# Merge-gate weights of a split-precision decoder block: the low half of every second weight tile by an accumulating DMA

## What is computed

```python
h = rmsnorm(x, g_norm)
z = einsum('bsd,dn->bsn', h, w_in)          # 16 heads' q/k/v/gate, forget logits, two merge gates
qa, ka, va, ga, qb, kb, vb, gb, fl, ma, mb = split(z)
...                                         # differential and forgetting attention, gated by SiLU
ya = einsum('bsw,wd->bsd', oa, w_proj_a)
yb = einsum('bsw,wd->bsd', ob, w_proj_b)
m = sigmoid(ma) * ya + sigmoid(mb) * yb
x = x + einsum('bsd,de->bse', m, w_out)
return rmsnorm(x, g_final)
```

## Time and profile before

| | |
|---|---|
| median of 3 runs | 762.3 us (762.3 to 762.76) |
| the profiled execution, its own time | 762.72 us |
| its span, first to last instruction | 760.9 us |
| PE busy | 751.2 us, 99% of the span |
| DVE busy | 422.1 us, 55% |
| ACT busy | 365.8 us, 48% |
| POOL busy | 76.3 us, 10% |
| bytes moved | 143.80 MB, 189 GB/s over the span |
| mean granted TensorE clock | 0.998 of full speed |

### The profile page before, as it was taken

How to read it: one execution, slowest core, us unless ns; L and a number is a source line. 1 busy time by engine, 2 the same in 40 slices (tenths; PEclk the granted TensorE clock), 3 DMA queues, 4 the chain that set the end, 5 groups by cost and what they waited for, 6 DMA issues and landing times.

```text
span 760.9 us, 9586 instructions
## 1 busy us (share of the span) xinstructions
PE 751.2 (99%) x3632; PEld 628.7 (83%) x3632; DVE 422.1 (55%) x616; ACT 365.8 (48%) x556; POOL 76.3 (10%) x153
## 2 busy tenths in 40 slices
PE   8999999999999999999999999999999999999996
PEld 6898888888888888888888888888888888888886
DVE  6754555555555566566665564444445666565552
ACT  6563554445544555445545554443444443444541
POOL 0001111101121221122202000000000000001110
PEclk9999999999999999999999999999999999999999
DMA  8747554554555545554545555555555555855642
GB/s 315 267 159 257 175 185 165 169 191 166 182 174 171 177 166 171 179 178 164 184 166 167 178 173 183 189 192 194 194 194 193 192 180 193 347 193 191 189 145 111
DMA packets 39885, 143.80 MB, mean 189 GB/s; under 512 B 4568, under 2 KB 4576, under 8 KB 39328
## 3 DMA queue, kind: packets, MB, share of 16 engines
q1 hardware_dynamic: 38576, 139.81, 54.8%
q10 hardware_dynamic: 1008, 1.84, 0.7%
q0 software_dynamic: 256, 1.54, 0.5%
HBM read 141.06 MB, written 2.11 MB: 188 GB/s over the span
## 4 chain that ended last, share of the span: by engine, by line
PE 96%; issue 1%; DMA 1%; DVE 0%; ACT 0%; DVEq 0%; POOLq 0%; POOL 0%; ACTq 0%
PE Z L219 29%; PE Z L221 29%; PE Z L220 29%; PE Z L340 3%; PE A L285 1%; PE A L253 1%; PE B L267 1%; PE Dk L276 1%; PE B L264 1%; DMA g_col<-in_g_cols 1%; PE C L294 0%; PE B L302 0%; PE A L302 0%; DVE w_lo L621 0%; ACT w_hi L422 0%
## 5 line engine op out<-in xcount | busy, mean ns | idle before, releaser
L621 DVE TENSOR_TENSOR w_lo<-w_raw,w_hi 128x1024 fp32r<-128x1024 f32 (+1 forms) x252 | 309.6, 1231 | 302.6 <-ACT w_hi L422 300.8
L422 ACT ACTIVATE w_hi<-w_raw 128x1024 fp32r<-128x1024 f32 (+1 forms) x247 | 261.6, 1060 | 348.2 <-PE Z L221 343.1
L219 PE MATMUL Z<-w_hi,hT_hi 128*128 128x512 f32 (+2 forms) x880 | 337.8, 384 | 0.4 <-DVE w_lo L621 0.4
L221 PE MATMUL Z<-w_hi,hT_lo 128*128 128x512 f32 (+2 forms) x880 | 335.3, 381 | 0.0
L220 PE MATMUL Z<-w_lo,hT_hi 128*128 128x512 f32 (+2 forms) x880 | 335.1, 381 | 0.0
L219 PEld LDWEIGHTS Z<-w_hi,hT_hi 128*128 128x128 f32 x880 | 165.4, 188 | 32.0 <-issue 0.6
L221 PEld LDWEIGHTS Z<-w_hi,hT_lo 128*128 128x128 f32 x880 | 165.4, 188 | 31.9
L220 PEld LDWEIGHTS Z<-w_lo,hT_hi 128*128 128x128 f32 x880 | 165.5, 188 | 30.5
L219 PE MATMUL Z<-w_hi,oT_hi 128*128 128x512 f32 x128 | 50.1, 391 | 0.0
L221 PE MATMUL Z<-w_hi,oT_lo 128*128 128x512 f32 x128 | 49.9, 389 | 0.0
L220 PE MATMUL Z<-w_lo,oT_hi 128*128 128x512 f32 x128 | 49.8, 389 | 0.0
(11 more groups left out here) (161 smaller groups left out, 485.2 us busy)
## 6 DMA issues: line engine op xcount, KB each, us to landing
w_raw<-in_w_main SPq DMA_DIRECT2D x251, 512.0 KB, 3.3
w_raw<-in_w_fl SPq DMA_DIRECT2D x4, 528.0 KB, 4.5
x_sb<-in_x SPq DMA_DIRECT2D x1, 2048.0 KB, 9.2
x_sb<-in_xT ACTq DMA_DIRECT2D x4, 256.0 KB, 7.4
x_sb<-in_xT SPq DMA_DIRECT2D x4, 256.0 KB, 5.6
rows<-c_rows_dram POOLq DMA_DIRECT2D x1, 1024.0 KB, 6.2
rows<-in_g_final SPq DMA_DIRECT2D x1, 1024.0 KB, 11.2
out_y<-gates SPq DMA_DIRECT2D x2, 384.0 KB, 2.5
```

Of the source, the lines that this page charges most:

```text
L219: pe.matmul(acc, a_hi, b_hi, start=first, stop=False)
L221: return pe.matmul(acc, a_lo, b_hi, start=False, stop=last)
L422: act.activation(w_hi[:, t % RING, 0:n], w_raw[:, t % RING, 0:n], ACT.Copy).then_inc(hi_ready, 1)
L621: dve.tensor_tensor(w_lo[:, t % RING, 0:n], w_raw[:, t % RING, 0:n], w_hi[:, t % RING, 0:n].bitcast(fp32), ALU.subtract).then_inc(lo_ready, 1)
```

## The change

For the tiles with `added(t)`, those with odd `t` from 129 to 191 (32 tiles, in slots 1 and 3 of the ring), DVE's subtraction is left out. ACT writes the high half as before and then the negated high half, `-w_hi` of the same rounding, into `w_lo`. GpSimd then issues a DMA that reads the tile from HBM a second time and adds it onto `w_lo`, so that `w_lo` becomes `w - w_hi`. PE waits for that DMA in place of `lo_ready`. SP waits for the negation (`neg_ready`) in place of DVE's subtraction before it reloads the raw slot. The counts of `lo_ready` are renumbered, since fewer tiles raise it.

```diff
+        neg_ready, lo_added = sem("neg_ready"), [sem("lo_added0"), sem("lo_added1")]
...
+        def added(t):
+            return 8 * MERGE <= t < 8 * PROJ and t % 2 == 1
+
+        def lo_count(t):
+            return sum(not added(i) for i in range(t + 1))
+
+        def add_count(t):
+            return sum(added(i) for i in range(t + 1))
...
             def load(t):
 
-                if t >= RING:
-                    sp.wait_ge(lo_ready, t - RING + 1)
+                if t >= RING and added(t - RING):
+                    sp.wait_ge(neg_ready, add_count(t - RING))
+                elif t >= RING:
+                    sp.wait_ge(lo_ready, lo_count(t - RING))
...
             def tile(t, pair, stat_hi, stat_lo, k0, ks, n, first, last):
                 pe.wait_ge(hi_ready, t + 1)
-                pe.wait_ge(lo_ready, t + 1)
+                if added(t):
+                    pe.wait_ge(lo_added[t % RING // 2], 16 * ((add_count(t) + 1) // 2))
+                else:
+                    pe.wait_ge(lo_ready, lo_count(t))
...
                 act.activation(w_hi[:, t % RING, 0:n], w_raw[:, t % RING, 0:n], ACT.Copy).then_inc(hi_ready, 1)
+                if added(t):
+                    act.activation(w_lo[:, t % RING, 0:n], w_raw[:, t % RING, 0:n], ACT.Copy, scale=-1.0).then_inc(neg_ready, 1)
...
             def split(t):
 
+                if added(t):
+                    return
                 dve.wait_ge(hi_ready, t + 1)
...
+            def add_low(tiles):
+
+                for t in tiles:
+                    if added(t):
+                        pool.wait_ge(neg_ready, add_count(t))
+                        pool.dma_start(w_lo[:, t % RING, 0:2 * CHUNK], w_main[t - 4],
+                                       accum_op=ALU.add).then_inc(lo_added[t % RING // 2], 16)
+
             for c in range(2, PROJ):
                 if 0 <= c - 2 < HEADS:
                     head_bias(c - 2)
                 if HEADS <= c - 1 < N_HEADS:
                     rope(c - 1)
+                add_low(range(8 * c + 4, 8 * c + 10))
                 if HEADS <= c - 3 < N_HEADS:
                     pool.wait_ge(o_ms_ready, c - 3 - HEADS + 1)
                     pool.tensor_tensor(o_rstd[:], o_ms[:], neg_half[:], ALU.pow).then_inc(o_rstd_ready, 1)
+                add_low(range(8 * c + 10, 8 * c + 12))
```

## The result

The changed kernel takes 795.64 us (793.94 to 796.74, four runs) against 762.3 us, a ratio of 1.0435 with a 95% interval of 1.042 to 1.045: 33.3 us slower. The direction was forecast, the size wasn't: 774 us, of a range of 762 to 812, is a loss of 11.7 us, and the loss is nearly three times that.

What follows compares the result with a forecast made beforehand. PE, busy throughout the merge chunks, was taken as the bound; removals and added engine work counted nothing, and the accumulating DMA's excess in the ring's turns summed to 11.6 us. Forecast: 762.3 + 11.7 = 774 us, range 762 to 812.

Steps and rivals of the forecast that it cites:

- Nothing to gain: Merge chunks: removing 32 DVE subtractions, 39 us of work lying beside PE's, takes away no PE wait; worth nothing.
- ACT, SP and POOL cost nothing: Merge chunks: 32 ACT copies, SP's raw slot release 0.3 us earlier and 32 POOL issues of about 0.56 us are hidden.
- The turn, and an excess paid once in each: Ring of four tiles, 10.88 us: landing time beyond 5.9 us is paid once per turn, two turns in each of eight chunks.
- L: Time of the accumulating DMA into `w_lo` from issue to landing; taken as 7.0 us, with 5.9 us available.
- the prediction's own sum: Merge chunks: excess per turn less PE's extra slack, 8.8 + 1.9 + 0.9 = 11.6 us.
- e: Excess of the accumulate's landing over the 5.9 us that the ring's turn leaves; taken as 1.1 us.
- the slack of PE's attention work: Extra slack per turn: 1.3 us in chunks 16 and 17, 0.65 in 18, 0.14 in 19, none in 20 to 23.
- I take L = 7.0, e = 1.1: Accumulate's landing in the ring: 6.2 us plus 0.8 for slower loads nearby, 1.1 us over the 5.9 available.
- the landing of `rows`: 1 MB load issued by POOL between raw loads, 6.2 us; taken as nearest to an accumulate, which also fetches 1 MB.
- The reading by the engines' time: DMA engines: two raw loads plus one accumulate need 92.4 engine-us against 87 per two tiles, 10.6 us over 32 pairs.
- the pace that I drew from it, 787 us: Rival, chance 0.15: an accumulate holds the DMA engines for 49.8 engine-us, a pair needs 99.6 against 87; 25 us lost.
- The estimate of 3.2 us for 512 KB: Skill page's time for a GpSimd DMA, 2.0 us plus bytes at 436 GB/s; by it nothing would be lost.

Runs made afterwards that it cites:

- few_columns: Changed kernel with each accumulating DMA bringing only 8 of the 1024 columns (rest left out of the computation): 762.14 us, ratio 0.9999 to the kernel before.
- plain_copy: Changed kernel with POOL's 32 DMAs as plain copies of the same 512 KB, without the addition: 762.51 us, ratio 1.0004 to the kernel before.
- one_in_four: Changed kernel with half as many added tiles, only t mod 4 = 1: one run 783.9 us, three 796.8 to 798.9 (profiled: 796.8); no ratio given.
- early_by_two: Changed kernel with the negation taken two tiles earlier, using four instead of two buffers for the added low halves: 764.49 us, ratio 1.0029 to the kernel before.
- raw_later: Changed kernel with the raw load into an added tile's slot also waiting for the next tile's high half: 769.62 us, ratio 1.0082 to the kernel before.
- traffic_only: Kernel before, DVE making all low halves, plus 32 accumulating DMAs of the same size and pace into a spare buffer: 762.05 us, ratio 0.9997.
- quiet_raw: Changed kernel with the raw loads of the merge chunks' even tiles cut to 8 columns: 794.06 us, ratio 1.0426 to the kernel before.
- quiet_all: Changed kernel with all raw loads of the merge chunks from tile 132 on cut to 8 columns: 765.32 us, ratio 1.0036 to the kernel before.
- traffic_together: traffic_only with each accumulate issued at the end of DVE's subtraction, together with the raw load into the same slot: 762.45 us, ratio 1.0 to the kernel before.
- neg_first: Changed kernel with ACT writing the negated high half before the high half, the latter releasing the raw slot: 774.64 us, ratio 1.0167 to the kernel before.
- early_by_one: As early_by_two, but with the negation one tile ahead and not two: 770.19 us, ratio 1.0104 to the kernel before.
- half_columns: Changed kernel with each accumulating DMA bringing 512 of the 1024 columns, 256 KB (others left out of the computation): 768.07 us, ratio 1.0073 to the kernel before.
- neg_first_raw_later: Changed kernel with both edits, negation ahead of the high half and raw load held until the next tile's high half: 768.48 us, ratio 1.0082.

## Why the size of the prediction was wrong

**Nothing to gain: right.** In few_columns all 32 subtractions are gone from DVE and the time is 762.14 us.

**ACT, SP and POOL cost nothing: right, with one omission.** few_columns and plain_copy have all of that work and lose nothing. The issue takes 0.86 us and not 0.56, inside the landing. POOL wakes 0.30 us after the negation; I named the waking and gave it no time, and it belongs in the turn.

**The turn, and an excess paid once in each: right.** The turn of the timeline above grew from 10.88 to 13.56 us, by 2.7 us for its two accumulates together. With the measured 8.0 + 0.3 us for L the prediction's own sum gives e = 2.4 and 8 x 2.4 + 2 x 2.3 + 2 x 1.75 + 4 x 1.1 = 31.7 us, 794 us, against 795.6. one_in_four, in its traced execution, has the same waiting with half of the DMAs, and early_by_two shows that a longer turn takes the loss away. PE's waits in chunks 16 and 17 are small, 0.3 to 0.9 us, and up to 2.4 later, as the slack of PE's attention work said.

**"I take L = 7.0, e = 1.1": the step that failed.** It is the term of the sum that was mis-sized: the landing measured 8.0 us, 8.3 with the waking, so e was 2.4 us and not 1.1, and the loss 33 us and not 11.7. I took the landing of `rows` and added 0.8 us for a stream that is always busy. The runs show that a busy stream isn't what matters: the landing is 5.7 us at a share of 0.98 (raw_later) and 6.7 at 0.99 (traffic_only), and 7.8 to 7.9 at 0.76 and 0.69 (quiet_raw, one_in_four). Alone it is 5.4 us, which would have fitted. What the changed kernel adds is 2.6 us of delay by one raw load: the diff moves the release of the raw slot from DVE's `lo_ready` to `neg_ready`, the very event that starts the accumulate. I priced that move on SP's side only, 0.3 us earlier, "no cost". quiet_raw against quiet_all, raw_later, and traffic_together against traffic_only show it from three sides.

**The reading by the engines' time.** I priced an accumulate at 42.6 engine-us; it is 49.4, two raw loads' worth. The Trainium skill ("Collectives: The Full Stack", section "The bandwidth ceiling: the fold count and why AG ≠ RS ≠ AR") says that a reduction reads two sources on the same side and halves the rate. The trace agrees: 342 ns for a packet against 161 for a plain one. (The 24.9 engine-us of a raw load in the prediction divide by 65 issues; by the bytes, 33.55 MB, they are 64 loads of 25.3, which changes nothing.) But the pace that I drew from it, 787 us, is refuted by traffic_only, 762 us with every byte: the engines' time per raw load wasn't the same in both kernels, 176 ns for a packet at a share of 0.56 and 149 at 0.99. The estimate of 3.2 us for 512 KB, by the fixed time plus bytes of the Trainium skill ("DMA: Bandwidth & Descriptors", section "Anatomy of one DMA — SWDGE (gpsimd) path"), is what 8 columns took here, and 1.3 us less than the plain 512 KB beside the raw loads.

**Near the edge the sum is too low.** With the median landing of each, it gives 768 us for neg_first, 763 for raw_later, 762 to 765 for early_by_one and 765 for half_columns; they measured 774.6, 769.6, 770.2 and 768.1. The landings spread over 2 to 3 us, and each that is late is paid while an early one earns nothing. That this is all of the difference isn't shown. In the changed kernel all were late and the median served.

**Where the delay comes about.** A raw load holds the engines for 24.4 / 16 = 1.5 us and yet delays the accumulate by 2.6 us. The traces hold the packets of each queue, and they tell part of the reason. Two accumulates, each with its raw load issued 0.27 us ahead: one_in_four's of 510.06 us with the full raw load, quiet_all's of 500.70 with the raw load of 8 columns. From 1.5 to 3.5 us after the issue, first one_in_four (511.56 to 513.56), then quiet_all (502.20 to 504.20):

```profile
q1 hardware_dynamic: 102, 0.35, 47.0%
q0 software_dynamic: 17, 0.07, 31.5%
```

```profile
q0 software_dynamic: 69, 0.28, 103.1%
```

Of the accumulate's 144 packets 17 are in the engines in the one and 69 in the other. Over all accumulates of a trace (medians), its packets begin 1.6 us after the issue in quiet_all and the last of them 4.7, and 2.5 and 7.3 in one_in_four. So the raw load puts off the beginning by 0.9 us and draws out the packets from about 3.1 to 4.8 us. plain_copy begins as late, 2.3 us after the issue, but its last packet begins at 3.9: its packets are half as long. In quiet_raw, where the next raw load is one of 4 KB, they begin at 2.6 and 7.2, so the bytes of the next raw load don't explain the drawing out.

**Open.** Why the packets are drawn out so far isn't settled, since the traces don't tell in which engine a packet ran. Nor is it settled which of the two raw loads ahead makes neg_first_raw_later's 7.0 us: its accumulates begin at 1.7 us, as raw_later's do at 1.6, and their last packets at 6.3 against 5.0.

## What to carry to other kernels

When a step of a ring is handed from an engine to a DMA, work out the turn: from the release of a slot to its next use, less every step on the way, the waking too. What is left is the longest landing that is free, and the latest landings decide, not the median. Look at what else the same event releases: two DMAs started by one semaphore meet in the same engines, and here the kernel gained by 26 us when the one that somebody waits for went first (raw_later). And an engine with idle time beside a PE that never waits has nothing to give: taking 37 us of work from DVE was worth nothing before any price was paid.

## What the runs showed of the hardware

An accumulating DMA of 512 KB holds the DMA engines for 342 ns for each of its packets, a plain one on the same queue for 161 (plain_copy). Most of its 4 KB packets last 0.33 us, but some 16 of the 128 about 0.7 (one_in_four).

PE's clock fell behind some of the gaps. In the changed kernel, after the longest wait, and then PE in the window of the slow matmuls (clock, DMA share and GB/s are the last three columns):

```profile
585.62 0.47 PE L231 MATMUL Z<-w_hi,hT_hi 128*128 128x512 f32 x1 [2.43 <-DMA w_lo<-in_w_main]
...
586.67 0.63 PE L231 MATMUL Z<-w_hi,hT_hi 128*128 128x512 f32 x1
587.09 0.63 PE L232 MATMUL Z<-w_lo,hT_hi 128*128 128x512 f32 x1
...
589.57 0.40 PE L232 MATMUL Z<-w_lo,hT_hi 128*128 128x512 f32 x1
```

```profile
586.20:589.20 3.00, 3.00 (x8) 0.50 0.98 209
```

The granted clock is 0.50 there and the matmuls start 0.42 to 0.43 us apart and not 0.227: half speed, the lower of the two levels, 1.2 and not 2.4 GHz, for some 3 us. It cost about 1.6 us here. There are six such stretches of 2.6 to 3.4 us in the merge chunks of the changed kernel (one), one_in_four (three) and quiet_raw (two), each after a wait of 2.2 to 2.5 us. Other waits of 2.2 to 2.5 us in the same profiles were followed by none, and so were all the shorter ones. The three in one_in_four cost about 5 us. That is less than half of the 13 us between its profiled execution and the one of 783.9 us; the rest isn't settled.
